# Weight halves by an accumulating DMA, a gate in three passes, and an earlier mean and variance in a two-block kernel

## The chip, the cores and the metric

One core of a Trainium2 chip runs the whole program. The metric is the device time of one execution in microseconds, as a median of three runs. A profiled execution of the same kernel gives the rows shown here.

## What is computed

Two transformer blocks on 256 tokens of width 1024, in fp32. The change lies in the first block's mixer: one wide input projection, a convolution module and a gated linear attention (GLA) branch, merged by two sigmoid gates. Behind it come an output projection, a mixture of 64 experts, and a second block that the change doesn't touch. Cut to what matters:

```python
def first_block(x, ...):
    h = x @ w_in + b_in
    conv_a, conv_g, q, k, v, r, f_lr, gate_a, gate_b = split(h)
    u = conv_a * sigmoid(conv_g)
    u = depthwise_causal_conv(u, conv_w, width=31) + conv_b
    u = silu(layer_norm(u, conv_ln_g, conv_ln_b))       # mean and variance over 1024 channels
    y_conv = u @ w_conv_out + b_conv_out
    y_gla = gla_branch(q, k, v, r, f_lr, ...) @ w_gla_out
    merged = sigmoid(gate_a) * y_conv + sigmoid(gate_b) * y_gla
    x = layer_norm(ALPHA * x + merged @ w_out + b_out)
    return layer_norm(ALPHA * x + hier_moe(x, ...))      # 64 experts, top 2
```

## The kernel before

The program is written engine by engine, each engine's instructions in the order in which they run, with semaphores between them. Activations lie transposed, 1024 channels as eight tiles of 128 partitions, 256 tokens wide. `w_in` comes in slabs of 512 columns (2 MB each) through a ring of four slots, loaded by SP in the order of `SLABS1`; a slot is loaded again when its slab has been used.

**Three passes.** For eleven slabs (`InSplit.SLABS`, g0 to ga1) the product is made in three passes of a faster matmul. A slab is cut into four units of 1024 columns a partition, numbered n = 0 to 43. ACT copies the weights of a unit into a rounded format (`high`, L527), DVE subtracts that from the weights and writes the rest (`low`, L532), and PE multiplies high by high, high by low, and low by high (`three_passes`, L454 to L456), 24 matmuls a unit. Three pairs of buffers are used in turn: ACT may write unit n when PE has read unit n - 3 (`wait_read`), and PE waits for the low of its unit (`wait_low`). ACT then takes the results of unit n - 3 out of PSUM (`outputs`, L823).

**DVE's loop.** `block1_dve` goes through the units: the low of unit n, now and then a step of the gate, the GLA state or the heads, and then a few taps of the convolution (`some_taps`, L987; 8 tiles x 31 taps = 248, one instruction each), whose number a unit is `pace`. Behind the loop `norm_heads` (L1048) scales the GLA heads, the semaphore "gla_conv" reaches "gla_in" (y is ready), the taps that are left run in one piece, and it reaches "conv_sum".

**PE behind the units.** The eight gb tiles (second gate) are made from the plain weights in fp32 by `pe_slab_tiles` (L367), then PE waits for "gla_in" and makes four go tiles (`w_gla_out`). It waits for "conv_sum" and makes the convolution norm's mean, a product with a matrix of 1/1024; DVE subtracts it (L1126), ACT squares (L913). PE makes two more go tiles, then the variance, then the last two. ACT takes the root (L462), DVE the reciprocal (L468) and the product (L1131), ACT the silu (L918). `act_parts` (L1108, L1109) splits its eight tiles into high and low for the eight `w_conv_out` tiles (co0 to co7) of `EndSplit`, which also work in three passes; `lows` (L590) makes the low halves of their weights, `gate_gla` (L1088) and `gate_conv` (L1094) multiply the gates in. The four units a slab of `w_out` follow, then the router, then the experts.

**Loads.** SP waits in its own order, so that what stands behind a wait waits too: the memory tokens wait for "gla_in" and ga7, then a gain, co0, and the first 4 MB expert slab (L1755), which waits for "moe_read0", set by PE behind ga1. Expert slabs follow as their places come free, and PE works through them as they land.

Of the kernel before, what the change touches and what calls it, by code (L numbers as in the profile page):

```python
# [230 lines left out]
class Chip:  # L231
# [114 lines left out]
    def rstd(self, i):  # L346

        return self.A(2, T, 1024 if i == 3 else 240 + T * i)

    def first_slab(self, ring):  # L350

        return self.ring_cols(ring.slot("a0") * SLOT_COLS, SLOT_COLS).rearrange("p (m k n) -> p m k n", m=4, k=DT)
# [133 lines left out]
class InSplit:  # L486

    SLABS = ["g0", "a1", "g1", "k", "v0", "v1", "q", "r0", "r1", "ga0", "ga1"]  # L490
    ROWS = ("k", "v0", "v1")
    BUFS = 3

    def __init__(self, K):
        self.K = K
# [5 lines left out]

    def part(self, n, low):
        k = 2 if self.SLABS[n // 4] in self.ROWS else DT
        return self.K.parts(12 + n % self.BUFS, 1024, 1024 * low).rearrange("p (k n) -> p k n", k=k)

    def source(self, eng, n):

        slab, i = self.SLABS[n // 4], n % 4
        w = self.K.slab(self.K.ring1.wait_landed(eng, slab))
        return w[:, 2 * i:2 * i + 2, :] if slab in self.ROWS else w[:, :, i * P:(i + 1) * P]  # L510

    def wait_read(self, eng, n):

# [20 lines left out]

    def wait_low(self, eng, n):

        eng.wait_ge(self.K.sem("in_low"), n + 1)


class EndSplit:  # L540
# [1 line left out]


    UNITS, CONV = 16, 8
    READ, FIRST = 3 * len(InSplit.ROWS), 4 * len(InSplit.SLABS)

    def __init__(self, K):
        self.K = K
# [44 lines left out]
def block1_pe(K, pe):  # L593
# [117 lines left out]
    for pair in range(2):  # L711
# [17 lines left out]
    pe_group(K, pe, B, "conv_mean", [K.c("j1024")] * DT, [conv[:, j, :] for j in range(DT)])  # L729
    pe_slab_tiles(K, pe, B, R, "go1", tiles("go", 4, 2), y, last=False)  # L730
    pe.wait_ge(S("conv_squares"), 1)
    pe_group(K, pe, B, "conv_var", [K.c("j1024")] * DT, [squares[:, j, :] for j in range(DT)])
    pe_slab_tiles(K, pe, B, R, "go1", tiles("go", 6, 2), y, first=2)
    end = EndSplit(K)
    for n in range(EndSplit.CONV):
        b = B.take(pe, f"co{n}")
        pe.wait_ge(S("in_low"), end.FIRST + n + 1)
# [11 lines left out]
    def project(t, s, i):  # L749

        n = EndSplit.CONV + 4 * s + i
        group = f"wo{t}_{s}"
        b = B.take(pe, group) if i == 0 else B.place[group][0]
        pe.wait_ge(S("in_low"), end.FIRST + n + 1)
# [61 lines left out]
def block1_act(K, act):  # L816
# [27 lines left out]
    def outputs(slab, i):  # L844

        if slab in ("g0", "g1"):
            m = i + 4 * int(slab[1])
            if m == 0:
                act.wait_ge(S("params_in"), 80)
            evac(f"g{m}", sg[:, m, :], ACT.Sigmoid, bias=K.v("b_g", m))  # L850
        elif slab == "k":
            if i == 0:
                act.wait_ge(S("ones_row"), 1)
                evac("f", K.f_low(), ACT.Identity, bias=K.vec[0:RANK, VEC["b_f"][0]:VEC["b_f"][0] + 1],
                     rows=slice(0, RANK))
            if i == 3:
                for t in range(TT):
                    evac(f"k_{t}", k[:, t, :], ACT.Copy, cols=slice(0, 512))
        elif slab == "q":

            if i == 0:
                act.wait_ge(S("q_bias"), 1)
            evac(f"q{i}", q[:, i, :], ACT.Identity, bias=K.q_bias()[:, i:i + 1], scale=float(P) ** -0.5)
        elif slab in ("v0", "v1"):
            n = int(slab[1])
            if n == 0 and i == 1:
                softplus()
            if i == 3:
                for t in range(TT):
                    evac(f"v{n}_{t}", v[:, t, 512 * n:512 * n + 512], ACT.Copy, cols=slice(0, 512))  # L870
        elif slab in ("r0", "r1"):
            m = i + 4 * int(slab[1])
            evac(f"r{m}", K.tiles(7, DT)[:, m, :], ACT.Silu, bias=K.v("b_r", m))
        elif slab in ("ga0", "ga1"):
            m = i + 4 * int(slab[2])
            evac(f"ga{m}", K.tiles(8, DT)[:, m, :], ACT.Sigmoid, bias=K.v("b_ga", m))


    kdec, o = K.tiles(10, TT, GDK, TT * GDK), K.tiles(4, DT)
# [26 lines left out]
    for m in range(DT):  # L906
        evac(f"gb{m}", K.tiles(9, DT)[:, m, :], ACT.Sigmoid, bias=K.v("b_gb", m))
    end = EndSplit(K)
    for n in (0, 1):
        end.high(L, n)  # L910
# [47 lines left out]
def block1_dve(K, dve):  # L958
# [89 lines left out]
        L.read(dve.tensor_tensor(heads, heads, rstd, ALU.mult), B, g)  # L1048

    for n in range(split.units):  # L1050
        split.low(L, n)
        done = n - split.BUFS
        pace = 0 if done < 0 else 2 if done < 4 or 8 <= done < 12 else 4
        if done == 0:
            dve.wait_ge(S("params_in"), 80)
            L.done(dve.tensor_scalar(K.q_bias(), K.v("b_q", 0, GH), float(P) ** -0.5, None, ALU.mult), S("q_bias"))
# [1 line left out]
            gate(done)  # L1058
        elif 8 <= done < 12:
            gate(done - 4)  # L1060
        if n == 22:
            log_decay()
        elif n == 27:
            keys_decayed()
        elif n in (30, 32, 34, 36):
            next_state((n - 30) // 2)
        elif n in (39, 40):
            for m in range(4 * (n - 39), 4 * (n - 39) + 4):
                gate_head(m)
            pace = 1  # L1070
        elif n == 41:
# [4 lines left out]
    for pair in range(2):  # L1076
        norm_heads(pair)
    dve.sem_inc(S("gla_conv"), 1)
    some_taps(range(DT), CW * DT)
    dve.wait_ge(taps, CW * DT)  # L1080
# [47 lines left out]
    for m in (4, 5):  # L1128
# [87 lines left out]
def block1_sp(K, sp):  # L1216
# [18 lines left out]
    def load(slab):  # L1235
# [4 lines left out]
            src = d[w][int(slab[2])]  # L1240
        before = R.before[slab]
        if before in InSplit.SLABS:
            split.wait_low(sp, split.unit(before) + 3)
# [254 lines left out]
def moe_act(K, act):  # L1498
# [3 lines left out]
    act.wait_ge(S("group_below"), 1)  # L1502
    for t in range(TT):
        L.done(act.activation(W.gexp[:, t, :], W.logits[:, t, 0:NG], ACT.Exp, bias=W.group_max[:, t:t + 1],
                              accum_out=W.gsum[:, t:t + 1]), S("group_exp"))
    act.wait_ge(S("expert_below"), 1)
    for t in range(TT):
        L.done(act.activation(W.eexp[:, t, :], W.masked[:, t, :], ACT.Exp, bias=W.expert_max[:, t:t + 1]), S("expert_exp"))
    for t in range(TT):
        L.done(act.activation(W.top2_exp[:, t, :], W.top8[:, t, 0:2], ACT.Exp, bias=W.expert_max[:, t:t + 1],  # L1510
                              accum_out=W.sums[:, t:t + 1]), S("expert_exp"))
# [196 lines left out]
    L.done(dve.tensor_scalar(u_rows[:, 1, :], x2[:, 1, :], K.stat("rstd", 1), None, ALU.mult), S("u_rows1"))  # L1708


def moe_pool(K, pool):

    S, B, W, L = K.sem, K.banks1, router_views(K), K.line("pool", pool)
    step, V = S("pool_steps"), moe_views(K)
    pool.wait_ge(S("group_exp"), TT)
    pool.wait_ge(S("expert_exp"), 2 * TT)
# [1192 lines left out]
def host_arrays(inputs):  # L2909
# [35 lines left out]
            by_cut[:, CUTS - 1] = pieces.reshape(NQ, P, SLAB_COLS)  # L2945
    w = a["w_in"][0]
    out["w_in"] = np.stack([by_partition(w[:, IN_COLS[n]:IN_COLS[n] + 512]) for n in IN_SLABS])
    out["w_in_first"] = np.stack([by_partition(w[:, O_A + m * P:O_A + (m + 1) * P]) for m in range(4)])
    out["w_in_f"] = by_partition(w[:, O_F:O_F + RANK])
    for n in ("w_conv_out", "w_gla_out", "w_out"):  # L2950
# [74 lines left out]
```

## Time and profile before

| | us |
|---|---|
| median of three runs (1693.39 to 1693.9) | 1693.7 |
| the profiled execution, its own time | 1691.89 |
| span of its instructions | 1689.8 |
| PE busy in the span | 1364.6 (81%) |
| DVE busy | 674.2 (40%) |
| ACT busy | 472.0 (28%) |

Times in the rows are microseconds from the span's start. "Idle before" is the time that an engine stood ahead of the instructions of a row, with what released it. PEclk is the granted clock of PE, as a share of 2.4 GHz.

### The profile page before, as it was taken

The numbers are of one execution on the slowest core, as the hardware profiler recorded it, in microseconds if no ns is written. First come the engines' busy times: TensorE is split into PE (matmuls) and PEld (weight loads), VectorE is DVE, ScalarE is ACT, GpSimd is POOL, SyncE is SP. The second block draws the span as 40 slices with busy tenths as digits, with TensorE's granted clock in tenths as the row PEclk, the third lists the DMA queues.
The fourth block names the chain that finished last, engine by engine and source line by source line (L and its number), as shares of the span: only waits on it lengthen the run. The fifth ranks groups of instructions, "written<-read, shape, count | busy, mean of one in ns | idle before, by whom it ended". The sixth has DMA issues, their size and how long they took to land.

```text
span 1689.8 us, 21326 instructions
## 1 busy us (share of the span) xinstructions
PE 1364.6 (81%) x8600; PEld 883.5 (52%) x8600; DVE 674.2 (40%) x1109; ACT 472.0 (28%) x682; POOL 59.0 (3%) x27
## 2 busy tenths in 40 slices
PE   8999999976656666665666667566799999999998
PEld 7789988522212212221221222122499999778887
DVE  5787979311101100110111011001367888655874
ACT  4454233401001001010010010010265764546653
POOL 0000000670000000000000000000000000000000
PEclk9999999988787978887888888788999999999999
DMA  9433555899999999999999999999944325474440
GB/s 359 156 138 138 218 204 245 353 431 430 432 431 431 431 433 433 431 431 432 433 433 431 431 432 433 431 432 431 419 165 150 139 71 197 167 258 175 179 174 25
DMA packets 50441, 530.79 MB, mean 314 GB/s; under 512 B 4276, under 2 KB 5556, under 8 KB 33862
## 3 DMA queue, kind: packets, MB, share of 16 engines
q1 hardware_dynamic: 50374, 529.86, 75.8%
q8 instruction: 46, 0.75, 0.2%
q14 instruction: 21, 0.17, 0.0%
HBM read 528.80 MB, written 1.05 MB: 314 GB/s over the span
## 4 chain that ended last, share of the span: by engine, by line
PE 51%; DMA 39%; DVE 6%; ACT 3%; issue 1%; SPq 0%; DVEq 0%; ACTq 0%
DMA shared<-in_w 37%; PE psum L454 6%; PE psum L456 6%; PE psum L455 6%; PE psum L1433 6%; PE psum L367 5%; PE psum L2222 4%; PE psum L1456 4%; PE psum L2223 2%; PE psum L1462 2%; PE psum L1404 2%; PE psum L2059 1%; DVE ring_parts L590 1%; DMA arena<-in_w 1%; PE psum L611 1%
## 5 line engine op out<-in xcount | busy, mean ns | idle before, releaser
L1433 PE MATMUL psum<-ring,arena 128*32 128x512 f32 x992 | 145.3, 739 | 86.8 <-DMA ring<-in_w 86.6
L1433 PE MATMUL psum<-shared,arena 128*32 128x512 f32 x1040 | 151.0, 726 | 61.5 <-DMA shared<-in_w 61.4
L1665 DVE TENSOR_TENSOR shared<-shared,psum 128x512 f32<-128x512 f32 x16 | 11.0, 688 | 462.3 <-PE psum L1433 462.3
L1456 PE MATMUL psum<-shared 128*32 128x512 f32 x512 | 89.5, 834 | 68.4 <-DMA shared<-in_w 68.4
L454 PE MATMUL psum<-parts 128*128 128x256 f32 (+1 forms) x424 | 136.5, 322 | 0.7 <-DVE parts L532 0.7
L455 PE MATMUL psum<-parts 128*128 128x256 f32 (+1 forms) x424 | 135.1, 319 | 0.0
L1433 PEld LDWEIGHTS psum<-ring,arena 128*32 128x32 f32 x992 | 34.3, 132 | 185.3 <-DMA ring<-in_w 100.2
L456 PE MATMUL psum<-parts,ring_parts 128*128 128x256 f32 x464 | 131.2, 283 | 0.0
L1433 PEld LDWEIGHTS psum<-shared,arena 128*32 128x32 f32 x1040 | 38.2, 129 | 168.3 <-issue 91.8
L456 PE MATMUL psum<-parts 128*128 128x256 f32 (+1 forms) x392 | 126.1, 322 | 0.0
L454 PE MATMUL psum<-parts,ring_parts 128*128 128x256 f32 x400 | 114.8, 287 | 0.4 <-ACT shared L2256 0.4
L455 PE MATMUL psum<-rowbuf_parts,ring_parts 128*128 128x256 f32 x400 | 113.1, 283 | 0.0
L2222 PE MATMUL psum<-parts 128*128 128x512 f32 x308 | 110.6, 398 | 1.3 <-DVEq L2788 1.3
L1667 DVE COPY shared<-psum 128x512 f32<-128x512 f32 x16 | 11.1, 692 | 246.6 <-PE psum L1456 246.6
L1456 PE MATMUL psum<-ring,shared 128*32 128x512 f32 x512 | 75.4, 742 | 40.0 <-DMA ring<-in_w 39.3
L1948 DVE TENSOR_TENSOR parts<-ring,parts 128x1024 fp32r<-128x1024 f32 x66 | 80.9, 1226 | 56.4 <-ACT parts L1941 54.1
L987 DVE SCALAR_TENSOR_TENSOR arena<-arena,vec 128x256 f32<-128x256 f32 x240 | 98.8, 478 | 2.0
L1533 ACT ACTIVATE arena<-psum 128x256 f32<-128x256 f32 x16 | 6.1, 384 | 320.5 <-PE psum L1443 320.5
L1537 ACT ACTIVATE shared<-psum 128x512 f32<-128x512 f32 x16 | 9.6, 597 | 294.2 <-PE psum L1456 294.2
L2223 PE MATMUL psum<-parts 128*128 128x256 f32 x352 | 91.6, 281 | 0.0
L1941 ACT ACTIVATE parts<-ring 128x1024 fp32r<-128x1024 f32 x66 | 70.0, 1061 | 74.0 <-PE psum L2224 41.1
L456 PEld LDWEIGHTS psum<-parts,ring_parts 128*128 128x128 f32 x464 | 88.9, 192 | 0.0
(343 smaller groups left out, 2347.4 us busy)
## 6 DMA issues: line engine op xcount, KB each, us to landing
shared<-in_w SPq DMA_DIRECT2D x47, 4096.0 KB, 32.4
ring<-in_w SPq DMA_DIRECT2D x47, 4096.0 KB, 32.4
ring<-in_w_in SPq DMA_DIRECT2D x19, 2048.0 KB, 8.7
ring<-in_w_ffn_gate_up SPq DMA_DIRECT2D x11, 2048.0 KB, 8.2
ring<-in_w_gate SPq DMA_DIRECT2D x8, 2048.0 KB, 7.9
ring<-in_w_ffn_down SPq DMA_DIRECT2D x5, 2048.0 KB, 7.8
ring<-in_w_out SPq DMA_DIRECT2D x4, 2048.0 KB, 8.6
shared<-in_w SPq DMA_DIRECT2D x6, 1024.0 KB, 28.8
```

Of the source, the lines that this page charges most:

```text
L367: m = pe.matmul(o, weights[k], acts[k], start=(k == 0), stop=(k == n - 1 and bias is None))
L454: pe.matmul(out, w[0], x[0], start=start, stop=False)
L455: pe.matmul(out, w[0], x[1], start=False, stop=False)
L456: return pe.matmul(out, w[1], x[0], start=False, stop=stop)
L987: ins = dve.scalar_tensor_tensor(conv[:, m, :], u[:, m, w:w + T], cw[:, m, w:w + 1], conv[:, m, :], ALU.mult, ALU.add)
L1404: m = pe.matmul(ps[:, bank, k % 4 * P:(k % 4 + 1) * P], V.x_rows[:, t, k * P:(k + 1) * P], V.sel[:, t, :], start=(t == 0), stop=(t == TT - 1))
L1433: m = pe.matmul(ps[slots, bank, :], V.picked[:, k, slots], w[e * len(w) // QUAD][:, e % (QUAD // len(w)), j, :], start=(k == 0), stop=(k = ...
L1456: m = pe.matmul(ps[slots, MOE_BANK["down"][c], :], V.hidden_t[:, f, slots], w(e), start=(f == 0), stop=(f == ET - 1))
L1941: L.done(L.eng.activation(self.shaped(n, 0), src, ACT.Copy), K.sem("unit_high"))
L1948: L.done(L.eng.tensor_tensor(self.shaped(n, 1), src, self.shaped(n, 0).bitcast(F32), ALU.subtract), K.sem("unit_low"))
L2222: pe.matmul(ps[:, b, :], w[0][:, k, :], sp.both[:, k, :, :], start=(k == 0), stop=False)
L2223: m = pe.matmul(ps[:, b, 0:T], w[1][:, k, :], sp.u[0][:, k, :], start=False, stop=False)
```

## The change

Four things are changed together, all in block 1.

1. gb0 and gb1 become slabs 12 and 13 of `InSplit`, so that they are made in three passes and there are 52 units. The expert weights' first place is released behind gb, not behind ga.
2. Four pairs of buffers instead of three. The low of every fourth unit (n = 3, 7, ... 51, the last of each slab) is no longer DVE's: ACT writes the rounded weights with a minus sign into the low buffer, ahead of the high half, and POOL issues a DMA that adds the plain weights to it from HBM (512 KB, `accum_op=add`). The weights of the slabs with whole columns lie in HBM so that a unit is in one piece a partition. SP loads a slab's place again when its last high and its last DVE low are done.
3. DVE gives a unit without a low six taps; `norm_heads` moves into the loop, at units 45 and 46.
4. The mean comes behind three go tiles, the variance behind five. On DVE the first two lows of `w_conv_out` move from ahead of the mean to behind the product with the reciprocal root, and the gates are spread anew.

Two semaphores of the router become one. The diff, cut:

```diff
-    SLABS = ["g0", "a1", "g1", "k", "v0", "v1", "q", "r0", "r1", "ga0", "ga1"]
+    SLABS = ["g0", "a1", "g1", "k", "v0", "v1", "q", "r0", "r1", "ga0", "ga1", "gb0", "gb1"]
-    BUFS = 3
+    BUFS, BY_DMA = 4, 3
+    LATE = 4 * SLABS.index("gb0")
...
+        slot = 12 + n % self.BUFS
+        if self.by_dma(n):
+            slot = 9 if n < self.LATE else 6
...
     def high(self, L, n):
...
+        if self.by_dma(n):
+            L.done(L.eng.activation(self.part(n, 1), src, ACT.Copy, scale=-1.0), self.K.sem("in_minus"))
         L.done(L.eng.activation(self.part(n, 0), src, ACT.Copy), self.K.sem("in_high"))
+
+    def add_low(self, pool, n):
+        slab, i = self.SLABS[n // 4], n % 4
+        pool.wait_ge(self.K.sem("in_minus"), n // self.BUFS + 1)
+        src = self.K.d["w_in"][IN_SLABS.index(slab)][:, 1024 * i:1024 * i + 1024]
+        pool.dma_start(self.part(n, 1).rearrange("p k n -> p (k n)"), src, accum_op=ALU.add)\
+            .then_inc(self.K.sem("low_added"), 16)
...
     def wait_low(self, eng, n):
+        if self.by_dma(n):
+            eng.wait_ge(self.K.sem("in_high"), n + 1)
+            eng.wait_ge(self.K.sem("low_added"), 16 * (n // self.BUFS + 1))
...
     slab_tiles("ga1", "ga", 4)
+    for s in range(2):
+        slab_tiles(f"gb{s}", "gb", 4 * s)
     pe.drain().then_inc(S("moe_read0"), FREED)
-    for s in range(2):
-        pe_slab_tiles(K, pe, B, R, f"gb{s}", tiles("gb", 4 * s, 4), x)
     pe.wait_ge(S("gla_conv"), GLA_CONV["gla_in"])
-    pe_slab_tiles(K, pe, B, R, "go0", tiles("go", 0, 4), y)
+    pe_slab_tiles(K, pe, B, R, "go0", tiles("go", 0, 3), y, last=False)
     pe.wait_ge(S("gla_conv"), GLA_CONV["conv_sum"])
     pe_group(K, pe, B, "conv_mean", ...)
-    pe_slab_tiles(K, pe, B, R, "go1", tiles("go", 4, 2), y, last=False)
+    pe_slab_tiles(K, pe, B, R, "go0", tiles("go", 3, 1), y, first=3)
+    pe_slab_tiles(K, pe, B, R, "go1", tiles("go", 4, 1), y, last=False)
     pe.wait_ge(S("conv_squares"), 1)
     pe_group(K, pe, B, "conv_var", ...)
-    pe_slab_tiles(K, pe, B, R, "go1", tiles("go", 6, 2), y, first=2)
+    pe_slab_tiles(K, pe, B, R, "go1", tiles("go", 5, 3), y, first=1)
...
     for n in range(split.units):                       # block1_dve
-        split.low(L, n)
+        by_dma = split.by_dma(n)
+        if not by_dma:
+            split.low(L, n)
-        pace = 0 if done < 0 else 2 if done < 4 or 8 <= done < 12 else 4
+        pace = 0 if done < 0 else 2 if done < 4 or 8 <= done < 12 else 6 if by_dma else 4
...
+        elif n in (45, 46):
+            norm_heads(n - 45)
+            pace = 1
...
-    for m in range(4):
+    for m in range(3):
         gate_gla(m)
-    lows(0, 2)
     b = B.wait_full(dve, "conv_mean")
     L.read(dve.tensor_tensor(conv, conv, wide(ps[:, b, 0:T], DT), ALU.subtract), B, "conv_mean")
...
     L.done(dve.tensor_tensor(conv, conv, wide(K.rstd(0), DT), ALU.mult), S("conv_normed"))
-    gate_gla(6)
+    lows(0, 2)
+    gate_gla(5)
     for m in range(DT):
         act_parts(m)
-    gate_gla(7)
+    for m in (6, 7):
+        gate_gla(m)
     lows(2, 4)
...
+def block1_pool(K, pool):
+    split = InSplit(K)
+    for n in range(split.BY_DMA, split.units, split.BUFS):
+        split.add_low(pool, n)
```

## Rows read from the trace of the kernel before

**Rows 1.** The page: its first line, and the shares of the chain that ended last.

```profile
span 1689.8 us, 21326 instructions
...
PE 51%; DMA 39%; DVE 6%; ACT 3%; issue 1%; SPq 0%; DVEq 0%; ACTq 0%
```

**Rows 2.** Stretches: length, busy PE, PEld, DVE, ACT, POOL, then PEclk, DMA share, GB/s.

```profile
10.00:30.00 20.00, 20.00 (x125) 18.58 (x124) 7.51 (x11) 7.52 (x8) 0.00 (x0) 1.00 1.02 422
...
21.64:56.40 34.76, 34.76 (x290) 34.67 (x288) 28.44 (x47) 16.28 (x19) 0.00 (x0) 1.00 0.76 305
...
183.92:211.52 27.60, 27.60 (x128) 24.32 (x129) 27.60 (x71) 3.64 (x8) 0.00 (x0) 1.00 0.70 263
211.52:225.30 13.78, 13.78 (x66) 12.13 (x65) 13.49 (x35) 3.88 (x4) 0.00 (x0) 1.00 0.54 232
...
245.97:251.60 5.63, 4.62 (x26) 3.35 (x25) 5.15 (x15) 5.43 (x8) 0.00 (x0) 1.00 0.78 279
251.60:272.00 20.40, 20.40 (x171) 20.19 (x169) 19.31 (x29) 9.95 (x14) 0.00 (x0) 1.00 0.19 79
```

**Rows 3.** Timeline of PE in unit 23: start, length, instruction, idle time before it.

```profile
97.12 0.50 PE L454 MATMUL psum<-parts 128*128 128x512 f32 x1 [0.68 <-DVE parts L532]
```

**Rows 4.** Timeline of DVE from the last unit to the first co tile.

```profile
182.05 42.05 DVE L987 SCALAR_TENSOR_TENSOR arena<-arena,vec 128x256 f32<-128x256 f32 x106
...
226.16 2.48 DVE L590 TENSOR_TENSOR ring_parts<-ring,rowbuf_parts 128x1024 fp32r<-128x1024 f32 x2
229.16 2.29 DVE L1126 TENSOR_TENSOR arena<-arena,psum 128x2048 f32<-128x2048 f32 x1 [0.52 <-PE psum L367]
...
240.09 1.75 DVE L468 RECIPROCAL arena<-arena 128x256 f32<-128x256 f32 x1 [3.61 <-ACT arena L462]
241.87 2.29 DVE L1131 TENSOR_TENSOR arena<-arena 128x2048 f32<-128x2048 f32 x1
...
244.90 0.29 DVE L1108 CAST parts<-shared 128x256 fp32r<-128x256 f32 x1 [0.28 <-ACT shared L918]
...
250.74 0.43 DVE L1109 TENSOR_TENSOR parts<-shared,parts 128x256 fp32r<-128x256 f32 x1
```

**Rows 5.** Groups by line in DVE's loop, 17 to 182 us: DVE's lows, ACT's highs.

```profile
L532 DVE TENSOR_TENSOR parts<-ring,parts 128x1024 fp32r<-128x1024 f32 x44 | 53.8, 1223 | 34.5 <-ACT parts L527 34.3
...
L527 ACT ACTIVATE parts<-ring 128x1024 fp32r<-128x1024 f32 x44 | 46.6, 1059 | 82.7 <-PE psum L456 75.9 <-DMA ring<-in_w_in 6.5
```

**Rows 6.** The same view: the stretch behind block 1.

```profile
299.70:1200.00 900.30, 600.63 (x3826) 210.48 (x3828) 97.61 (x200) 75.41 (x116) 58.78 (x23) 0.84 1.00 430
```

**Rows 7.** Timeline of SP's DMA issues between 183 and 300 us.

```profile
183.75 0.38 SPq L1258 DMA_DIRECT2D shared<-in_mem  x1
...
198.46 0.35 SPq L1755 DMA_DIRECT2D shared<-in_w  x1
...
298.75 0.33 SPq L1768 DMA_DIRECT2D rowbuf<-in_w  x1
```

**Rows 8.** The same view: two idle stretches of PE and what follows each.

```profile
356.97:362.38 5.41, 0.00 (x1) 0.01 (x1) 0.00 (x0) 0.60 (x1) 5.31 (x2) 0.88 1.00 430
362.38:367.87 5.49, 5.49 (x28) 1.37 (x32) 0.00 (x0) 0.00 (x0) 4.93 (x7) 0.50 1.01 436
...
444.00:450.04 6.04, 0.00 (x1) 0.01 (x1) 0.00 (x0) 0.00 (x0) 0.00 (x0) 0.70 0.99 420
450.04:453.20 3.16, 3.16 (x16) 0.77 (x20) 0.00 (x0) 0.00 (x0) 0.00 (x0) 0.50 1.01 436
```

**Rows 9.** Timeline of ACT: the squares and the root of the variance.

```profile
231.54 1.91 ACT L913 ACTIVATE arena<-arena 128x2048 f32<-128x2048 f32 x1 [15.70 <-DVEq L1127]
239.51 0.47 ACT L462 ACTIVATE arena<-psum,con 128x256 f32<-128x256 f32 x1 [6.06 <-PE psum L367]
```

**Rows 10.** DMA issues, two short stretches: KB, us from issue to landing.

```profile
arena<-in_x_rows SPq DMA_DIRECT2D x1, 1024.0 KB, 4.9
...
ring<-in_w_in SPq DMA_DIRECT2D x1, 2048.0 KB, 9.0
```

More of the change, by code:

```diff
@@ L348, in rstd, with first_slab_at @@
         return self.A(2, T, 1024 if i == 3 else 240 + T * i)
+    def first_slab_at(self, slot):
+        return self.ring_cols(slot * SLOT_COLS, SLOT_COLS).rearrange("p (m k n) -> p m k n", m=4, k=DT)
     def first_slab(self, ring):
-        return self.ring_cols(ring.slot("a0") * SLOT_COLS, SLOT_COLS).rearrange("p (m k n) -> p m k n", m=4, k=DT)
+        return self.first_slab_at(ring.slot("a0"))
     def slab(self, slot, k=DT):
@@ L503, in part, with by_dma, lows @@
         k = 2 if self.SLABS[n // 4] in self.ROWS else DT
-        return self.K.parts(12 + n % self.BUFS, 1024, 1024 * low).rearrange("p (k n) -> p k n", k=k)
+        slot = 12 + n % self.BUFS
+        if self.by_dma(n):
+            slot = 9 if n < self.LATE else 6
+        return self.K.parts(slot, 1024, 1024 * low).rearrange("p (k n) -> p k n", k=k)
+    def by_dma(self, n):
+        return n % self.BUFS == self.BY_DMA
+    def lows(self, n):
+        return n + 1 - (n + 1) // self.BUFS
     def source(self, eng, n):
         slab, i = self.SLABS[n // 4], n % 4
-        w = self.K.slab(self.K.ring1.wait_landed(eng, slab))
-        return w[:, 2 * i:2 * i + 2, :] if slab in self.ROWS else w[:, :, i * P:(i + 1) * P]
+        slot = self.K.ring1.wait_landed(eng, slab)
+        if slab in self.ROWS:
+            return self.K.slab(slot)[:, 2 * i:2 * i + 2, :]
+        return self.K.first_slab_at(slot)[:, i]
     def wait_read(self, eng, n):
@@ L535, in wait_low @@
     def wait_low(self, eng, n):
-        eng.wait_ge(self.K.sem("in_low"), n + 1)
+        if self.by_dma(n):
+            eng.wait_ge(self.K.sem("in_high"), n + 1)
+            eng.wait_ge(self.K.sem("low_added"), 16 * (n // self.BUFS + 1))
+        else:
+            eng.wait_ge(self.K.sem("in_low"), self.lows(n))
 class EndSplit:
     UNITS, CONV = 16, 8
-    READ, FIRST = 3 * len(InSplit.ROWS), 4 * len(InSplit.SLABS)
+    READ, FIRST, FIRST_LOW = 3 * len(InSplit.ROWS), 4 * len(InSplit.SLABS), 3 * len(InSplit.SLABS)
     def __init__(self, K):
@@ L736, in block1_pe @@
         b = B.take(pe, f"co{n}")
-        pe.wait_ge(S("in_low"), end.FIRST + n + 1)
+        pe.wait_ge(S("in_low"), end.FIRST_LOW + n + 1)
         w = end.part(n, 0), end.part(n, 1)
@@ L753, in project @@
         b = B.take(pe, group) if i == 0 else B.place[group][0]
-        pe.wait_ge(S("in_low"), end.FIRST + n + 1)
+        pe.wait_ge(S("in_low"), end.FIRST_LOW + n + 1)
         w = end.part(n, 0), end.part(n, 1)
@@ L876, in outputs @@
             evac(f"ga{m}", K.tiles(8, DT)[:, m, :], ACT.Sigmoid, bias=K.v("b_ga", m))
+        elif slab in ("gb0", "gb1"):
+            m = i + 4 * int(slab[2])
+            evac(f"gb{m}", K.tiles(9, DT)[:, m, :], ACT.Sigmoid, bias=K.v("b_gb", m))
     kdec, o = K.tiles(10, TT, GDK, TT * GDK), K.tiles(4, DT)
@@ L904, in block1_act @@
                    B, "o_ms")
-    for m in range(DT):
-        evac(f"gb{m}", K.tiles(9, DT)[:, m, :], ACT.Sigmoid, bias=K.v("b_gb", m))
     end = EndSplit(K)
@@ L1060, in block1_dve @@
             gate(done - 4)
-        if n == 22:
+        if n == 23:
             log_decay()
-        elif n == 27:
+        elif n == 28:
             keys_decayed()
[L1065 to L1068, printed above, removed]
+        elif n in (31, 33, 35, 37):
+            next_state((n - 31) // 2)
+        elif n in (40, 41):
+            for m in range(4 * (n - 40), 4 * (n - 40) + 4):
                 gate_head(m)
             pace = 1
-        elif n == 41:
+        elif n in (45, 46):
+            norm_heads(n - 45)
+            pace = 1
+        elif n == 42:
             B.wait_read(dve, "o_ms")
@@ L1075, in block1_dve @@
             some_taps(range(min(done + 1, 4) if done < 8 else min(done - 3, DT)), pace)
-    for pair in range(2):
-        norm_heads(pair)
     dve.sem_inc(S("gla_conv"), 1)
@@ L1127, in block1_dve @@
     dve.sem_inc(S("gla_conv"), 1)
-    for m in (4, 5):
+    for m in (3, 4):
         gate_gla(m)
@@ L1242, in load @@
         if before in InSplit.SLABS:
-            split.wait_low(sp, split.unit(before) + 3)
+            last = split.unit(before) + 3
+            sp.wait_ge(S("in_high"), last + 1)
+            sp.wait_ge(S("in_low"), split.lows(last))
         elif before:
@@ L1504, in moe_act @@
         L.done(act.activation(W.gexp[:, t, :], W.logits[:, t, 0:NG], ACT.Exp, bias=W.group_max[:, t:t + 1],
-                              accum_out=W.gsum[:, t:t + 1]), S("group_exp"))
+                              accum_out=W.gsum[:, t:t + 1]), S("router_exp"))
     act.wait_ge(S("expert_below"), 1)
     for t in range(TT):
-        L.done(act.activation(W.eexp[:, t, :], W.masked[:, t, :], ACT.Exp, bias=W.expert_max[:, t:t + 1]), S("expert_exp"))
+        L.done(act.activation(W.eexp[:, t, :], W.masked[:, t, :], ACT.Exp, bias=W.expert_max[:, t:t + 1]), S("router_exp"))
     for t in range(TT):
         L.done(act.activation(W.top2_exp[:, t, :], W.top8[:, t, 0:2], ACT.Exp, bias=W.expert_max[:, t:t + 1],
-                              accum_out=W.sums[:, t:t + 1]), S("expert_exp"))
+                              accum_out=W.sums[:, t:t + 1]), S("router_exp"))
     act.preload_act_table(ACT.Sqrt)
@@ L2947, in host_arrays @@
     out["w_in"] = np.stack([by_partition(w[:, IN_COLS[n]:IN_COLS[n] + 512]) for n in IN_SLABS])
+    for i, n in enumerate(IN_SLABS):
+        if n not in InSplit.ROWS:
+            out["w_in"][i] = out["w_in"][i].reshape(P, DT, 4, P).transpose(0, 2, 1, 3).reshape(P, SLOT_COLS)
     out["w_in_first"] = np.stack([by_partition(w[:, O_A + m * P:O_A + (m + 1) * P]) for m in range(4)])
```

4 lines of the change are left out of this document (2 added, 2 removed).

## The prediction

> **What bounds the kernel now.** I read the page's head and its chain first. The span is 1689.8 us, and the chain that ended last is half PE and more than a third DMA [rows 1]. The windows by stage come next [rows 2]. PE is busy without a break in the stretches from 21 us to 246 us, at the full granted clock. Twelve units of the input projection (three slabs) take 34.6 us, 2.88 us a unit. The eight gb tiles in plain fp32 take 27.6 us, 3.45 us a tile. The four tiles of go0 take 13.8 us, the same rate. PE loses time in two places: before unit 23, where it stands for 0.68 us [rows 3], and in the first w_conv_out tile, 245.97 to 251.60, which takes 5.6 us where the others take 2.9 us [rows 2]. That tile waits for act_parts on DVE [rows 4].
>
> The third view is DVE's. In the loop over the units it follows PE: before its lows it stood 34.3 us, all waiting for ACT's high halves, and ACT in turn stood 75.9 us waiting for PE to read a buffer [rows 5]. After the loop it runs 106 taps in one piece, from 182.05 to 224.1 us, 0.397 us each [rows 4]. So "conv_sum" comes at 224.1, and PE reaches the mean behind four go tiles at 225.3 [rows 2]. The two are in step.
>
> The last view is what follows. From 299.7 to 1200 us the DMA engines are full, 430 GB/s at a share of 1.00 [rows 6]. That stream begins with a load at 298.75, which waits for the output projection's end [rows 7], so a microsecond at the end of block 1 is a microsecond at the end of the kernel. What decides is when the w_conv_out tiles start.
>
> **The change part by part.** Times below are on the clock of the profiled execution.
>
> *gb in three passes.* 8 x 2.88 = 23.0 us takes the place of 27.6 us. PE is done with gb at 183.6 + 23.0 = 206.7 rather than 211.5, a gain of 4.6 us on PE. It holds if the lows of the eight units are there in time; the six that DVE makes are ready some 6 us ahead (192.3 + 1.1 + 1.3 for low 50, whose unit PE begins at 201), since four buffers let it run that far.
>
> *Lows moved off DVE.* 11 of the 44 old units go to the transfer, 6 of the 8 new ones come to DVE: 5 fewer at 1.25 us, so 6.3 us of DVE work is gone. ACT gets 13 more passes of 1.06 us [rows 5]; two of them are 2.1 us of a unit's 2.88 us and an evacuation of half a microsecond fits beside them, so they hide, apart from the stretch after softplus.
>
> *Where that DVE time goes.* This is the step that decides. The taps in the loop are counted out: with the new pace (2, 4 or 6 a unit, 1 at four of them) I count 184 before the loop ends, and 64 after it (142 and 106 before). The loop cannot end before PE has read unit 46, for low 50 waits for high 50 and that for this buffer. Unit 46 is read at 183.6 + 3 x 2.88 = 192.3. Then come high 50 (193.4), low 50 (194.7), four taps (1.6 us) and the six of unit 51 (2.4 us): 198.7. So "gla_in" is set at 198.7, in time for PE at 206.7, and 64 x 0.397 = 25.4 us later, at 224.1, "conv_sum". That is where it is now. The 6.3 us become more standing in the loop: four units of PE's pace are 11.5 us, and DVE has three lows and eighteen taps for them, 3 x 1.25 + 18 x 0.397 = 10.9 us.
>
> *The mean behind three go tiles.* PE is there at 206.7 + 0.3 + 3 x 3.45 = 217.3. It waits until 224.2, 6.9 us, with everything behind it. The gain on gb ends in this wait.
>
> *The clock after the wait.* The trace has no wait of this length in block 1. Bounds come from the nearest rows: after idle stretches of 5.4 and 6.0 us in the expert stage PE came back at 0.50 of the clock, the 1.2 GHz level, and stayed there for 5.5 and 3.2 us [rows 8]. At half rate that costs 1.6 to 2.8 us. Below nothing it can't go; I take 2.2 us, the middle, as this wait is longer than both.
>
> The Trainium skill, "TensorE: Matmul & The Clock Gate", section "Part 1: The HAM clock gate", says the same against this change: a PE left idle drops to the throttled state and has to earn the full clock back by activity. If its rule did not hold here, the sum below would be 2.2 us less.
>
> *From the mean to the first w_conv_out tile.* Mean: 224.2 + 3.45 + 2.2 = 229.9 (before: 228.8). Centring 0.3 + 2.3, squares on ACT 0.1 + 1.9: 234.5, in time. PE's two go tiles end at 236.8 and the variance at 240.25 (before: 239.1). Square root 0.9 us, reciprocal and product 1.8 + 2.3: 245.2 [rows 4, 9]. Here stands what the new order adds: two lows (2.5 us), which lay in a gap before the mean, and the gate of go5 (0.46 us) now come between the product and act_parts: 248.2. act_parts is eight steps of 0.79 us: 254.5, and the tile ends some 0.4 us later, at 254.9 instead of 251.6. That is 3.3 us late, of which 1.2 us are there without the clock. The gates of go6 and go7 (one more than before) stand ahead of the next lows, so DVE, busy 19.3 of the next 20.4 us [rows 2], is 3.7 us late.
>
> *Unit 23.* Its low came late from DVE; by the transfer PE's stand of 0.7 us before it [rows 3] may go, which moves the whole loop. It holds if the transfer takes under 6 us there, as ACT issues its minus late after softplus. So 2.6 to 3.7 us late, and I take 3.1.
>
> *The accumulating transfer.* The trace has none, nor any DMA from POOL. Its time, from ACT's minus to the landing, has a limit: high n waits for the read of unit n - 4, three units before PE needs n, 3 x 2.88 = 8.64 us, less 1.2 us for the minus: 7.4 us. Units 7, 11 and 23 have just this or less; the others have other PE work in between. Rows that bound it: 1024 KB in rows of 4 KB landed in 4.9 us alone, as many bytes as 512 KB read and the 512 KB that it is added to; a 2048 KB slab landed in 9.0 us [rows 10]. And a slab load goes out with nearly each of these transfers, as the same unit's high half frees its slot. Sharing the engines evenly by bytes, the transfer is done when 1 MB to 2 MB have gone, 4.9 to 7.4 us; taking turns row by row with the slab's rows, four times as long, it ends with the slab, 9.0 + 1.2 = 10.2 us. I take 4.9 to 7.4: in time, hidden behind three units.
>
> The Trainium skill's "DMA: Bandwidth & Descriptors" has two rules here. In "Anatomy of one DMA — SWDGE (gpsimd) path" it fits 2.0 us and the bytes at 436 GB/s, 3.2 us for 512 KB as an estimate, well in time. In "Issuing engines are not separate DMA queues" it says that transfers from all engines run on the same 16 DMA engines and interleave, which speaks for the long end. No run here shows either for a POOL transfer; by the first the sum stays, by the second it is the first rival.
>
> *Queues.* On SP, mem, a gain and co0 wait for "gla_in" at 198.7 rather than for ga7 at 183.7; co0 goes out at some 200 us. The first expert slab waits for the drain behind gb, 207 instead of 198.5 [rows 7], and co1 behind it. All three have 20 us and more until they are read. On POOL nothing else is queued before 300 us. The merged router semaphore costs nothing.
>
> **The sum.** 1691.89 us is the profiled execution's own time; its median without profile is 1693.7, 1.8 us more. 1693.7 + 3.1 = 1696.8, say **1697** (+0.2%), between 1695 and 1699.
>
> **The rivals.**
>
> *The transfers land late.* For: the slab load beside each of them, and DMA engines that are full from 10 to 30 us [rows 2], when the first ones go out. Against: half a megabyte in rows of 4 KB. It decides at 7.4 us. At 9 us units 7, 11 and 23 stand 1.6, 1.6 and 2.6 us, and the loop's end and "conv_sum" move with them; 0.7 us of this was there before: 5 us on top of the 3.3, 1702; at 8 us 1699, at 10.2 us 1706.
>
> *DVE hands over early, and the change is faster.* If DVE's saved 6.3 us come out at its end rather than in the loop, "conv_sum" is there at 217.8, when PE is. Then there is no wait and no slow clock: mean 221.3, variance 231.6, product 236.7, act_parts 246.0, and the tile ends at 246.4, 5.2 us early: 1688.5. It decides at 217.3. Against it: DVE's 34.3 us of waiting in the loop, which this change doesn't shorten.
>
> *PE comes back from the wait at full clock.* 3.1 - 2.2 = 0.9 us late: 1694.6.
>
> **How the numbers follow.** Chances: my forecast 0.45, late transfers 0.32, early DVE 0.15, full clock 0.08. A difference of 0.2%, 3.4 us, is about what a measurement of this kernel can tell from none. The bound lies at 1697.1, inside my forecast's own 1695 to 1699, so of its 0.45 I give 0.20 to slower and 0.25 to the same. Slower: 0.20 + 0.31 = 0.51. The same: 0.25 + 0.08 + 0.01 = 0.34. Faster: 0.15. The range reaches to 1704, leaving out the late transfers' far end (0.10), and down to 1689, leaving out half of the early case (0.07).
>
> **What would show it.** In the changed kernel's trace: 64 taps in one piece, ending near 224; PE standing some 7 us ahead of the mean, at about 217, released by DVE; the granted clock at 0.5 for a few us behind it; two lows between the product and act_parts; the first w_conv_out tile ending at 253 to 256; no stand of PE at units 7, 11 and 23. If PE stands there, the transfers are late. If the taps end near 217, the prediction is wrong at the loop's end.

## The result and the profile after

The changed kernel takes 1714.4 us (median of 4 runs, 1711.4 to 1717.2), the kernel before 1693.6 us beside it: ratio 1.0125, interval 1.0112 to 1.0137, so 20.8 us slower. The prediction was 1697.0 us with a range from 1689 to 1704. The profiled execution took 1716.24 us, with a span of 1714.5.

Four lines of the page of the changed kernel: the queue that is new, the chain of work by engine, the three-pass matmuls (busy, mean ns | idle before them and what ended it), and the new issue (KB each, median us from issue to landing).

```profile
q0 software_dynamic: 1872, 6.82, 2.5%
PE 46%; DMA 43%; DVE 6%; ACT 4%; issue 1%; SPq 0%; DVEq 0%; ACTq 0%
L458 PE MATMUL psum<-parts 128*128 128x256 f32 (+1 forms) x488 | 159.1, 326 | 16.9 <-DMA parts<-in_w_in 15.6
parts<-in_w_in POOLq DMA_DIRECT2D x13, 512.0 KB, 8.4
```

L458 is the first of the three passes (L454 before). It now has 15.6 us of waiting for the transfers; before, the only stand in the loop was the 0.68 us of [rows 3]. The longest waits of PE up to 320 us, with those of the output projection (L621) among them (in total, times, longest):

```profile
PE psum L458 <- DMA parts<-in_w_in: 15.6, 5, 6.7
PE psum L642 <- DMA arena<-in_x: 6.7, 1, 6.7
PE psum L458 <- DVE ring_parts L621: 2.0, 3, 1.0
PE psum L458 <- ACT parts L546: 1.3, 1, 1.3
```

None of them is for the taps: PE never waited ahead of the mean. There the taps end at 243.0, and PE comes at 244.9:

```profile
213.65 29.39 DVE L1019 SCALAR_TENSOR_TENSOR arena<-arena,vec 128x256 f32<-128x256 f32 x74
```

The long stands on transfers are at units 3, 7, 11, 43 and 51, from 31.45, 47.21, 61.51, 193.27 and 222.34 us. The row puts the one at unit 11 down to ACT (the 1.3 us), as a high half ended at 62.97; but that is unit 14's, high 11 was done at 55.42, and the transfer landed at 62.94, just before PE went on at 63.08. The fifth wait of the first row is unit 23's, at 108.94 us: 0.56 us, for a transfer that landed at 109.75. PE's table by stretches shows three of the long stands with what follows, and the two stages behind gb (columns: length, busy time, granted clock, DMA share, GB/s):

```profile
31.45:34.26 2.81, 0.28 (x3) 1.00 1.02 404
34.26:38.80 4.54, 4.54 (x25) 0.62 1.00 429
193.27:196.79 3.52, 0.28 (x4) 0.86 0.69 229
196.79:202.63 5.84, 5.84 (x27) 0.50 0.01 2
222.34:229.34 7.00, 0.28 (x3) 0.80 0.83 302
229.34:233.35 4.01, 4.01 (x19) 0.50 0.03 6
234.47:268.89 34.42, 34.42 (x161) 1.00 0.70 275
268.89:294.12 25.23, 24.35 (x195) 1.00 0.32 125
```

Behind the stands at units 3, 43 and 51 PE works on at half the clock, the 1.2 GHz level; behind those at 7 and 11 (2.7 and 1.45 us) it doesn't. From unit 0 to gb's end the sum is: unit 0 begins 1.1 us later (22.76, 21.64 before); PE stands 17.0 us more (17.8 against the 0.8 ahead of unit 23, counted from one matmul's start to the next, less the usual distance); slow matmuls, most of them at half clock, take 9.2 us more (the excess of each interval over the median of its form, summed: 12.8 against 3.6); three passes for gb save 4.6. Of the 9.2 us, 6.0 lie right behind those three stands; most of the other 3.2 is two stretches at 0.50, from 72.9 and from 100.2 us, a little behind runs of small matmuls, with no stand just ahead of them, and whether the stands brought these too is open. Together 22.7, and gb ends at 234.4 instead of 211.5. From there to the end of w_conv_out it takes 1.2 us less than before. The load that begins the full stream goes out at 320.87 instead of 298.75 [rows 7], 22.1 us later.

### The profile page after: what moved, and what is told of

It is laid out like the page before. It is cut to its first block, busy times and chain, and to the rows that moved or that the text cites. A ratio compares the mean times of both kernels' runs of the same rounds, so it can differ in the third digit from the quotient of the medians.

```text
span 1714.5 us, 21509 instructions
## 1 busy us (share of the span) xinstructions
PE 1367.6 (80%) x8664; PEld 888.4 (52%) x8664; DVE 668.0 (39%) x1104; ACT 494.0 (29%) x703; POOL 70.4 (4%) x40
## 4 chain that ended last, share of the span: by engine, by line
PE 46%; DMA 43%; DVE 6%; ACT 4%; issue 1%; SPq 0%; DVEq 0%; ACTq 0%
DMA shared<-in_w 37%; PE psum L458 6%; PE psum L1471 6%; PE psum L459 6%; PE psum L460 6%; PE psum L2266 4%; PE psum L1494 4%; DMA parts<-in_w_in 3%; PE psum L2267 2%; PE psum L1500 2%; PE psum L371 2%; PE psum L1442 2%; PE psum L2103 1%; DVE ring_parts L621 1%; PE psum L2237 1%
## 5 line engine op out<-in xcount | busy, mean ns | idle before, releaser
L458 PE MATMUL psum<-parts 128*128 128x256 f32 (+1 forms) x488 | 159.1, 326 | 16.9 <-DMA parts<-in_w_in 15.6
L459 PE MATMUL psum<-parts 128*128 128x256 f32 (+1 forms) x488 | 157.1, 322 | 0.0
L460 PE MATMUL psum<-parts 128*128 128x256 f32 (+1 forms) x456 | 147.9, 324 | 0.0
L1494 PE MATMUL psum<-shared 128*32 128x512 f32 x512 | 90.2, 839 | 66.6 <-DMA shared<-in_w 66.6
L458 PE MATMUL psum<-parts,ring_parts 128*128 128x256 f32 x400 | 114.8, 287 | 0.4 <-ACT shared L2300 0.4
L458 PEld LDWEIGHTS psum<-parts 128*128 128x128 f32 x488 | 97.4, 200 | 27.2 <-issue 21.8
L1705 DVE COPY shared<-psum 128x512 f32<-128x512 f32 x16 | 11.1, 691 | 249.0 <-PE psum L1494 249.0
L459 PEld LDWEIGHTS psum<-parts 128*128 128x128 f32 x488 | 97.3, 199 | 5.5
L460 PEld LDWEIGHTS psum<-parts 128*128 128x128 f32 x456 | 91.1, 200 | 5.7
## 6 DMA issues: line engine op xcount, KB each, us to landing
ring<-in_w_in SPq DMA_DIRECT2D x19, 2048.0 KB, 11.1
```

The source lines that it names most:

```text
L458: pe.matmul(out, w[0], x[0], start=start, stop=False)
L459: pe.matmul(out, w[0], x[1], start=False, stop=False)
L460: return pe.matmul(out, w[1], x[0], start=False, stop=stop)
L1494: m = pe.matmul(ps[slots, MOE_BANK["down"][c], :], V.hidden_t[:, f, slots], w(e), start=(f == 0), stop=(f == ET - 1))
```

## The experiments

Each row has the median, that of the kernel before in the same comparison, their ratio with its interval, and the time at which the load goes out that begins the full stream (298.75 before), which measures block 1 alone. Where it says "one run", the time is that of a single execution, without an interval.

| run | us | before | ratio | load |
|---|---|---|---|---|
| the changed kernel | 1714.4 | 1693.6 | 1.0125 (1.0112 to 1.0137) | 320.87 |
| e1, loads held | 1703.1 | 1692.8 | 1.0059 (1.0042 to 1.0076) | 309.85 |
| e2, third unit by transfer | 1707.8 | 1692.8 | 1.0093 (1.0076 to 1.0110) | 314.92 |
| e3, few bytes | 1697.3 | 1692.8 | 1.0030 (1.0017 to 1.0042) | 301.77 |
| e4, no addition | 1697.1 | 1692.8 | one run | 304.09 |
| e5, loads held, first low by DVE | 1698.5 | 1691.8 | 1.0037 (1.0025 to 1.0050) | 304.68 |
| e6, e5 in the old order | 1696.1 | 1691.8 | 1.0021 (1.0011 to 1.0031) | 301.50 |
| e7, e5 with 28 matmuls in the wait | 1699.0 | 1691.8 | 1.0038 (1.0024 to 1.0052) | 307.23 |
| e8, e5 with more taps in the loop | 1690.9 | 1691.8 | 0.9997 (0.9987 to 1.0006) | 298.86 |
| e9, e8 without those at unit 12, two lows ahead | 1686.5 | 1692.3 | 0.9960 (0.9947 to 0.9974) | 293.69 |
| e10, e5 with 14 matmuls in the wait | 1693.3 | 1692.3 | 1.0003 (0.9994 to 1.0013) | 302.12 |
| e11, the kernel before again | 1690.2 | 1692.3 | one run | 299.36 |
| e12, e9 without transfers | 1689.6 | 1692.4 | 0.9984 (0.9975 to 0.9993) | 294.99 |

Ahead of the experiments, the trace tells what one late transfer looks like. The DMA window from the issue for unit 11 to PE's going on:

```profile
q1 hardware_dynamic: 90, 1.47, 41.9%
q0 software_dynamic: 144, 0.52, 41.6%
ring<-in_w_in SPq DMA_DIRECT2D x1, 2048.0 KB, 10.2
parts<-in_w_in POOLq DMA_DIRECT2D x1, 512.0 KB, 8.3
```

ACT's minus ended at 54.33, POOL issued at 54.62, SP issued the next slab at 55.45, the transfer's first packet began 1.6 us behind its issue, the slab's packets came in from 4.3 us on, and the last of the 128 packets ended at 7.4. Landing was 8.3 us behind the issue, 8.6 behind the minus, where the prediction's threshold was 7.4: PE stood 1.45 us. For units 3, 7, 43 and 51 landing took 12.8, 9.6, 12.2 and 13.7 us.

**e1, e2: away from the slab load.** e1:

```diff
             sp.wait_ge(S("in_low"), split.lows(last))
+            sp.wait_ge(S("low_added"), 16 * (last // split.BUFS + 1))
...
     sp.wait_ge(S("gla_conv"), GLA_CONV["gla_in"])
+    sp.wait_ge(S("low_added"), 16 * (split.units // split.BUFS))
```

> The changed kernel, but SP issues each load of a slab (and, behind the last transfer, the loads of mem, a gain and co0) only when the accumulating transfer of the same unit has landed. Theory (the transfer shares the DMA engines by bytes with the load that is released by the same unit): from POOL's issue to landing 6.2 us, as unit 47's was with nothing beside it, instead of 8.4 to 13.7; PE stands at unit 3 alone (its neighbours were issued earlier), not at 7, 11, 43 and 51; 14 us of stands and some 8 us of half clock behind them go; 1696 to 1702 us. Rival A (POOL's issue and the accumulation themselves are what is slow): landing stays at 8 us or more, the stands stay, 1710 us or more. Rival B (the loads come late): landings fall to 6.2 us, but PE or ACT stands for slabs, over 1703 us.

e2 sets BY_DMA to 2, with the count of DVE's lows and the buffers to suit.

> The changed kernel, but the third of each four units goes by transfer, not the fourth, so that the transfer is issued one unit (2.88 us) ahead of the slab load. Theory (sharing with that load): the transfer has the DMA engines nearly to itself, 6.2 to 6.6 us from issue to landing, no stand of PE but at the first one; 1696 to 1702 us, as the run with held loads. Rival A (the transfer itself is slow): landing 8 us or more, the same stands one unit earlier, 1710 us or more.

From e1's trace, the transfers' landing (min/median/max) and who waits for them, and the window of unit 43's:

```profile
  PE psum L458: 3.9, 1
DMA to landing us min/median/max: 5.9/6.1/13.3
q0 software_dynamic: 144, 0.52, 55.0%
parts<-in_w_in POOLq DMA_DIRECT2D x1, 512.0 KB, 5.9
```

Alone, a transfer lands in 6 us; only the first, behind loads issued at 6.4 and 6.9 us, took 13.3. So the loads beside it cost 2.3 us of the median 8.4, and more where there were several. The stands at 7, 11, 43 and 51 went, and with them half of the loss: 10.4 us above before instead of 20.8. The time is 1 us above what was expected, as the stand at unit 3 grew to 4.1 us, with half clock behind it. It also lies just over the 1703 of rival B, and ACT did stand 8.1 us for the load of co0; but behind that it waited 13.2 us for DVE before the squares, and PE waited for no load, so the path does not go through it. e2 has the same landings (median 6.2 us) but not the same time: PE stood 4.0 us at unit 2 and 2.0 at unit 22, whose minus comes late, behind softplus, and 8.3 us ahead of the mean. Its landings fit the theory; its expected time of 1696 to 1702 was wrong.

**e3, e4: bytes, and the addition.** e3 cuts the transfer to `[:, 1024 * i:1024 * i + 64]`, e4 drops `accum_op=ALU.add`.

> The changed kernel with transfers of 64 of the 1024 columns (256 bytes a row in place of 4 KB, the same 128 rows); the other columns of these low halves are left without their addition. Theory (bytes): landing some 3 to 4 us after the issue, no stand of PE at these units, and what is left is the rest of the change as the prediction had it: PE behind gb at 207 to 209, a wait of 5 to 7 us ahead of the mean, half the clock behind it, the first w_conv_out tile's end 2 to 4 us later than before; 1696 to 1699 us. Rival A (fixed costs of a POOL transfer): landing 7 us or more and 1705 us or more. Rival C (the rest of the change costs too): no stands, but over 1702 us.

> The changed kernel with plain transfers, which overwrite in place of adding: the subtraction of the high halves is left out. Theory (sharing by bytes): the same 512 KB beside the same loads, landing 7 to 8.4 us, the stands all there or shorter by under 1.5 us each, 1706 to 1716 us. Rival A in its second form (the addition is slow): landing 5 to 6 us, packets shorter by a third or more, and no stand but at units 3 and 51, under 1704 us.

Landings in e4, and its window of unit 47's transfer, which had nothing beside it:

```profile
DMA to landing us min/median/max: 4.0/4.2/11.6
q0 software_dynamic: 144, 0.52, 48.5%
parts<-in_w_in POOLq DMA_DIRECT2D x1, 512.0 KB, 4.2
```

Here the theory fell short, and the second form of rival A was right for most units. Beside the same slab loads a plain transfer lands in 4.2 us: its last packet ends 3.6 to 3.9 us behind the issue, and the slab's begin at 2.8 to 3.2. In packet times: 48.5% of 16 engines over 4.10 us is 31.8 us for 128 packets, 0.25 us each; in e1 it is 55.0% over 6.14 us, 0.42 us each. POOL's issue takes 0.53 us plain and 0.86 us adding. So the addition costs some 2 us by itself, and these 2 us carry the transfer into the slab load, which costs 2.3 more. Only units 3 and 51 stay late in e3 and e4. In e3 the 32 KB of unit 51 took 11.1 us to land among the loads of mem, a gain and co0 that gla_in had just released: there it is the loads that count, not the transfer's bytes. e3's time lies in what was expected, but in part by luck: PE stood 4.2 us at unit 51 instead of waiting 5 to 7 us ahead of the mean, where it stood 1.2 us.

**e5: what is left of the prediction.** e1, with unit 3's low by DVE:

```diff
-        return n % self.BUFS == self.BY_DMA
+        return n % self.BUFS == self.BY_DMA and n > self.BY_DMA
```

> The run with held loads, and besides the low half of unit 3, the first one, by DVE again (its transfer landed 13.3 us after its issue, behind the first loads, and PE stood 4.1 us and then worked some 2.4 us longer at half the clock). Theory (the late transfers are all that the prediction's sum lacked): no stand of PE in the loop over the units, 6 to 6.5 us less than the 1703.1 us with held loads, so 1696 to 1698 us, which is the prediction's own sum; PE still stands some 7 us ahead of the mean, and half clock follows. Rival C (the rest of the change costs more than the sum says): 1700 us or more.

PE by stretches, one in the loop and those behind gb, and under them DVE's taps in one piece:

```profile
88.00:93.50 5.50, 5.50 (x15) 0.74 0.19 70
...
209.22:219.44 10.22, 10.22 (x47) 1.00 1.06 443
219.44:226.62 7.18, 0.38 (x3) 0.80 0.98 420
226.62:230.37 3.75, 3.75 (x9) 0.50 0.97 415
252.66:277.89 25.23, 24.34 (x195) 1.00 0.32 125
```

```profile
197.11 29.40 DVE L1019 SCALAR_TENSOR_TENSOR arena<-arena,vec 128x256 f32<-128x256 f32 x74
```

No stand in the loop (landings 5.9 to 6.4 us), and the wait ahead of the mean is there. It is 1698.5 us, half a microsecond above the range expected, and 6.7 above before, where the prediction's sum was 3.1. The account is in the next section.

**e6: the order alone.** In e5, mean and variance go back to their places, and two lows back ahead of the mean.

> The run before (held loads, first low half by DVE), with the mean again behind four go tiles, the variance behind six, and two low halves again ahead of the mean on DVE. By the prediction's terms: the wait ahead of the mean shrinks from 6.9 to 3.4 us, the half clock behind it goes or halves, act_parts begins 3 us earlier, and the time is 3 to 5 us below the run before: 1692 to 1694 us. Rival D (the order does not matter, as DVE sets the end of both): within 1 us of it.

The wait was 3.5 us, as expected, but half clock followed it too (0.55 over 3.70 us), and the first w_conv_out tile lost 2.8 us as in the kernel before. Block 1 ends 3.2 us earlier than in e5, the medians differ by 2.4. Rival D is out, the size was taken too high.

**e7, e10: the clock behind the wait.** In e5, ahead of the wait for conv_sum:

```diff
+    b = B.take(pe, "conv_mean")
+    for _ in range(28):                     # e10: 14
+        pe.matmul(K.psum[:, b, 0:T], K.c("ident"), K.con[:, CON["after"][0]:CON["after"][0] + T], start=True, stop=True)
     pe.wait_ge(S("gla_conv"), GLA_CONV["conv_sum"])
...
```

> Held loads, first low half by DVE, and 28 matmuls of 216 ns (6.0 us, their result is overwritten) in the wait ahead of the mean. If the half clock behind that wait costs what the prediction says: 1.3 to 2.2 us less than the run without them, and the granted clock stays at 1.00 through the mean. Rival E (that clock hides behind DVE's chain): no difference over 0.5 us.

> Held loads, first low half by DVE, and now 14 plain fp32 matmuls in the wait ahead of the mean. In the run with 28 each of them showed as two of 216 ns, 12.1 us in all, 5 us longer than the wait; 14 are 6.05 us and fit. If the half clock behind the wait is on the path: PE runs the mean at 1.00 and the time is 1.5 to 2.1 us below the run without them (1698.5 us). Rival E (it hides behind DVE's chain): no difference over 0.5 us.

e7 was mis-sized: each plain fp32 matmul is two of 216 ns in the trace, 12.1 us in all, so that the mean began 4.6 us later than in e5, and nothing could be gained. e10, the matmuls, the rest of the wait and the mean:

```profile
219.09:225.14 6.05, 6.05 (x29) 1.00 0.93 398
225.14:226.05 0.91, 0.16 (x2) 1.00 1.01 432
226.05:229.60 3.55, 3.55 (x16) 1.00 0.95 406
```

The mean runs at 1.00 and takes 3.55 us, where e5 took 5.51, 1.96 us longer; block 1 ends 2.6 us earlier, 0.6 of it from an earlier conv_sum. Rival E is out. The median fell by 5.2 us; the part over 2.6 is not in block 1. In the traces, which differ by 7.0 us, 3.5 of it is in the last stage, from the experts' last matmul to the end, which takes 478.8 us in e10 and 482.3 in e5, but also 480.4 and 478.6 in the two traces of the kernel before. Why is open.

**e8, e9, e12: DVE's time at its end.** e8 and e9 change e5's loop on DVE; e9 also puts `lows(0, 2)` behind `gate_gla(0)`, ahead of the mean:

```diff
+        pace += {12: 12, 16: 4, 19: 8, 24: 4, 31: 2, 35: 2, 36: 6, 39: 5, 40: 4}.get(n, 0)   # e8
+        pace += {16: 4, 19: 8, 24: 4, 31: 2, 35: 2, 36: 6, 39: 5, 40: 4}.get(n, 0)           # e9
         if done >= 0:
             some_taps(
```

> Held loads, first low half by DVE, and 47 more taps inside DVE's loop, at the units where DVE waits longest for ACT (12 at unit 12, 4 to 8 at eight others). If DVE's saved time can be brought out at its end (the prediction's second rival): some 24 taps behind the loop, conv_sum at about 209 us, no wait of PE ahead of the mean, no half clock behind it, 1687 to 1691 us, faster than both kernels. Rival F (the taps push the low halves and PE stands in the loop): 1695 us or more.

> The run with more taps in the loop, without its 12 extra taps at unit 12 (PE stood 1.5 us there behind DVE, and then worked 1.6 us longer at half the clock), and with the two low halves of w_conv_out again ahead of the mean, where DVE has now some 10 us to wait. Theory (what is left of the loss is DVE's order, and the start): the stand and its half clock go, 3 us; act_parts begins 2.5 us earlier, so that the 1.7 us which PE lost in the first w_conv_out tile shrink to under 0.5; 3 to 4.5 us less than the run with more taps, 1686.5 to 1688.5 us beside 1691.8 of before. Rival G (such stands and dips only move to other places): 1690 us or more.

**e11: the kernel before again**, for the start of block 1.

> The kernel before once more, for its start: in every changed kernel so far PE began the first three-pass unit at 22.3 to 23.8 us, in the trace of before at 21.64. If that is of the change, this run begins at 21.6 again, with the full clock granted by about 9.5 us; if it varies from run to run, it begins anywhere from 21.6 to 23.8 us.

PE began unit 0 at 22.3 us, so the start differs by 0.7 us between the two traces of the kernel before; the changed kernels reach from 22.3 to 23.8.

**e12: without transfers.** It is e9 with `by_dma` always false, four taps at each of those units, and no loads held.

> The run with more taps and with two low halves ahead of the mean (1686.5 us), but without any transfer: all 52 low halves by DVE, 4 taps at each of the units that had 6, and loads held by nothing. Theory (the transfer's worth is DVE's time): 12 more low halves of 1.23 us, 24 taps more behind the loop, so conv_sum at 221 to 224 us where PE is at the mean by some 219.5; PE waits 2 to 4 us and may lose 1 to 2 us of clock: 1689 to 1692 us. Rival H (DVE has room in its waits for these as well): within 1 us of 1686.5 us, and the transfers weren't needed.

e9: the go tiles with mean and variance, and the w_conv_out tiles; and its taps behind the loop:

```profile
209.57:243.99 34.42, 34.42 (x160) 1.00 0.85 358
243.99:267.75 23.76, 23.38 (x195) 1.00 0.34 133
```

```profile
197.46 15.54 DVE L1019 SCALAR_TENSOR_TENSOR arena<-arena,vec 128x256 f32<-128x256 f32 x39
```

With 39 taps in one piece instead of 74 the sum is there at 213, PE goes from go through mean and variance without a gap, and act_parts is no longer late. e9 is 5.8 us faster than the kernel before, as was expected. e8, also inside what was expected, can't be told from before: its extra taps at unit 12 made PE stand 1.5 us, to 63.2, and PE had half clock from 66.6 to 70.0 us. e12 shows what the transfers are worth when they are on time: 3.0 us of e9's 5.8; the other 2.8 are there without any transfer. Its PE stands 1.5 us ahead of the mean, at full clock afterwards.

## Why the prediction was wrong

**The step that failed is the accumulating transfer.** Its term in the sum was nothing, as it was taken at 4.9 to 7.4 us from ACT's minus, in time; it is 6.4 alone (e1's median) and 8.5 to 10.0 beside a slab load (8.6 at unit 11), and 12.5 to 14.0 where more loads went out beside it. Two things were mis-sized. The bounds came from plain loads by counting the bytes of an addition twice; a plain 512 KB from POOL lands in 4.2 us, and adding makes each 4 KB packet 0.42 instead of 0.25 us. And the slab load does not share from the start: beside an adding transfer its packets come in 3.9 to 4.3 us behind POOL's issue, when about half of the transfer's packets are done; beside a plain one they come at 2.8 to 3.2, and the plain transfer's last packet ends by 3.9. The threshold itself held: 8.6 - 7.4 is 1.2 us, against a stand of 1.45 at unit 11.

By the fit in the Trainium skill's "DMA: Bandwidth & Descriptors", section "Anatomy of one DMA — SWDGE (gpsimd) path", 512 KB take 3.2 us, an estimate; measured were 4.2 us plain (e4) and 6.1 adding (e1), from issue to landing. The Trainium skill says on the same page, section "Issuing engines are not separate DMA queues", that transfers of all engines run on the same DMA engines and interleave. This agrees with 8.4 us beside a load and 6.1 without.

**The rival named it but priced it at 8 us in all, not 21.** First, units 3, 43 and 51 were missing. "The others have other PE work in between" is wrong for 47 and 51, which have the same 7.3 us from minus to need (in e1) as 7 and 11; 43 has 9.3 us, and its transfer took 12.5. The three stood 3.4 (43), 0 (47) and 6.9 us (51), since gla_out with the router's loads went out beside 43, mem with a gain and co0 beside 51, and nothing beside 47 (6.2 us). Unit 3 came behind the first loads. Second, the price of half clock stood behind the mean's wait only. Three stands in the loop brought it too: 6.0 us on top of the 17.0 that PE stood. Third, the rival kept the wait ahead of the mean and moved "conv_sum" with the stands; in the changed kernel PE stood at unit 51 instead, and that wait and its half clock are not there.

**The rest, read from e5, where the transfers are on time.** Point by point:

- 64 taps behind the loop: 74 in one piece, less the 4 of unit 50 and the 6 of unit 51 that stand ahead of it, is 64. Right.
- The wait ahead of the mean, 6.9 us: 6.96. Half clock behind it, 2.2 us: 1.96, from e5's 5.51 us for the mean against e10's 3.55. Both right, and e10 shows that it is on the path.
- The new order, two lows ahead of act_parts: the first w_conv_out tile still loses 1.7 us to act_parts (2.8 before), and e6 gives 3.2 us for undoing order and places together. Right in kind.
- Unit 23's stand goes: right in e5. In the changed kernel it stayed, 0.7 us by starts as against 0.8 before, now for the transfer: it landed 8.6 us behind its minus, and PE needed it after 7.9 (6.3 in e4, which has no half clock just there).
- The sum of 3.1 us: block 1 of e5 is 5.9 us late. 1.6 of it is that unit 0 begins at 23.27, and 1.6 that PE runs 88.0 to 93.5 at 0.74 of the clock, where e11, the kernel before again, has 1.00:

```profile
88.00:93.50 5.50, 5.50 (x23) 1.00 0.02 9
```

   The remaining 2.7 is the sum. In the two traces of before, unit 0 begins at 21.64 and 22.3, in those of the changed kernels at 22.3 to 23.8; how much of the late start and of the dip belongs to the change was not settled. The dip is also there in e12, without transfers, and not in e2, e3 and e4, which have the change. So it is in part luck that e5's 1698.5 lies inside the prediction's 1695 to 1699.
- PE at the full granted clock from 21 to 246 us: wrong for a stretch of the kernel before that no row of the prediction covers, where it was 0.55. The row below has it (length, busy PE, PEld, DVE, ACT, POOL, then the clock). The changed kernel has one like it, from 175.3 to 178.7 us, so it takes no part in the difference.

```profile
162.70:166.50 3.80, 3.80 (x21) 3.80 (x21) 2.46 (x6) 1.55 (x2) 0.00 (x0) 0.55 0.75 317
```

- The queues of SP: in the changed kernel nothing waited for a load that went out late. Where the loads are held, ACT waited for co0 (8.1 us in e1, 7.8 in e5), and then longer for DVE, and PE waited for no load.

**DVE handing over early** was given 0.15 and needs more than the change does: the time that DVE saves went into waits, as the prediction said. e9 got it out by putting 35 more taps where DVE waits, and there the gain is real. PE coming back from the wait at full clock did not happen: it came back at 0.50 in e5.

## What to carry to other kernels

Price a transfer by what else the same event releases: here one unit's pass on ACT started both the accumulating transfer and the slab load, and holding the load, which PE did not wait for, gave 10 us. Time saved on an engine that waits inside its loop comes out at the end only if work from behind the loop is moved into the waits. A stand of PE can cost half clock behind its length; price both for each stand, not for the longest alone.

## What was not expected of the hardware

- An adding DMA of 128 x 4 KB takes 0.42 us a packet and 6.1 us to land (e1), a plain one 0.25 us and 4.2 us (e4); POOL's issue 0.86 against 0.53 us.
- In e3, 32 KB in rows of 256 bytes took 11.1 us to land at unit 51 while 3.7 MB of other loads moved, and 2.3 to 3.2 us at ten other units.
- Behind PE's waits of 0.9 (e10), 1.5 (e12), 2.6 (unit 51 in e4) and 2.7 us (unit 7) the clock stayed at 1.00. Behind those of 2.7 (unit 3), 3.4 (unit 43), 3.5 (e6), 6.9 (unit 51) and 7.0 us (e5) it was 0.50. Some time after a stand of 1.5 us in e8, at 163 us of the kernel before and near 90 us in several runs (e5 and e12 among them) it was 0.50 too, with no long wait just ahead.
- The last stage takes 478.6 to 482.7 us with the same instructions in all traces, two of the same kernel among them 1.8 us apart.
